# Holding back the first loads of SP's queue and moving four weight steps one to two page units later, in a one-core decoder step

## The chip, the cores and the metric

The kernel runs on one core of a Trainium2 chip. The metric is the device time of one execution in microseconds. One core has five engines with instruction streams of their own: PE (TensorE), DVE (VectorE), ACT (ScalarE), POOL (GpSimd) and SP (SyncE). SP and ACT issue transfers on hardware queues, POOL on a software queue (q0 in the profile). SP's queue is q1, ACT's is q10. All queues share the core's 16 DMA engines.

## The reference

One decoder layer for a prompt of 512 tokens and eight samples of 8 tokens, model width 1024, fp32. The part that matters here is its start:

```python
mod = silu(c) @ w_ada + b_ada                    # (9 rows, 6*1024): three pairs of shift, scale and gate
h = rmsnorm(x, ln1_g) * (1 + scale) + shift      # x: 512 + 64 tokens x 1024
q, k, v, ... = split(h @ w_in)                   # the projection
kc = compress(cache_k_cmp[page_table])           # 8 samples x 16 pages, k and v
     # per 16 rows: chunk @ w_ck1 -> silu -> @ w_ck2
```

Behind it come attention in three branches, a short convolution, the output projection and a SwiGLU block, which the change doesn't touch.

## The kernel before, in words

**The start.** The paged keys and values of the compression branch are 16 *page units* of 1 MB (eight samples, keys and values in turn). POOL gathers each unit with four indirect transfers of 256 KB (line 894) into one of four slots of the ring `cring` in the tile `arena`; a slot is free when DVE has transposed the unit that lay in it (`turned`). For each unit u, DVE transposes it (line 1608), PE multiplies it by the first compression weights (`compress_first`, line 2521, 16 records of 128x256), ACT copies half of the product, DVE adds the other half, ACT applies silu, and PE multiplies by the second weights (`compress_second`, line 2529), for which it comes back after the next unit's first product. PE's order is a list written out by hand in a loop over the 16 units: `compress_first(u)`, then whatever the tables hang on this unit, then `compress_second(u - 1)`.

**What hangs on the units.** `ADA_AT` names the unit behind whose first product PE does step kk of the product of silu(c) with the first 2048 columns of `w_ada` (`ada_step`, line 2482, eight steps of 128 rows, each reads one 1 MB block). `X_AT` names the units at which PE turns the five normalised token tiles (`turn_tokens`, line 2447): tiles 0 and 1 at unit 8, 2 and 3 at unit 9, 4 at unit 10. At unit 12 PE turns the finished modulation (`mod_turn`). DVE then modulates the tokens and the projection begins at 114 us.

**SP's queue.** SP is a list in program order, too. It first loads the five token tiles (four of 512 KB, one of 256 KB, line 768), then the eight 1 MB blocks of `w_ada` (line 720) into the four slots of the ring `wring`, then the blocks of `w_in` (line 752) into the same slots. `cache(sp, i)` makes SP wait until page unit i has landed; it is a means of ordering only, since no data pass from the pages to these loads. Blocks 0 to 3 of `w_ada` wait for a page unit each. The bias (256 KB, line 760) goes out behind block 3. Blocks 4 to 7 have no `cache` wait; block 4 + n waits until PE has done step n (`ada_read`) and its slot is free, and the first four blocks of `w_in` wait for steps 4 to 7 in the same way. The squares of the token tiles are taken on ACT at units 2 to 6.

The first block of `w_in` is cast by ACT (line 534) at unit 13.

Of the kernel before, what the change touches and what calls it, by code (L numbers as in the profile page):

```python
# [54 lines left out]
    [0, 128, 8, 80, 16, 512, 124, 124, 256, 512, 32, 900, 128]).tolist()  # L55


ADA_AT = {4: 0, 5: 1, 6: 2, 7: 3, 8: 4, 9: 5, 10: 6, 11: 7}


ADA1_AT = {2: 0, 3: 1, 5: 2, 6: 3, 8: 4, 9: 5, 11: 6, 13: 7}
# [196 lines left out]
def decoder_kernel(nc, a, o):  # L258
    at = plan_banks()
    chunks = plan_weights()  # L260
    chunk_of = {k: i for i, (k, _) in enumerate(chunks)}

    with ExitStack() as ctx:
# [213 lines left out]
        def ps(key):  # L477
            return bank[at[key][0]]

        def want_free(eng, key):  # L480

            b, n = at[key]
            if n:
                eng.wait_ge(bank_free[b], n)
# [11 lines left out]
        def fills(ins, key):  # L496
            ins.then_inc(bank_filled[at[key][0]], 1)
# [10 lines left out]
        def weights(pe, key):  # L508

            i = chunk_of[key]  # L510
            pe.wait_ge(w_loaded[i % WR], sum(loads_of(j) for j in range(i % WR, i + 1, WR)))
            return wch[:, i % WR]
# [5 lines left out]
        def cache(eng, i):  # L518

            eng.wait_ge(cache_loaded[slot_of(i)], 64 * (i // CR + 1) if i < 16 else 256 + 16 * (i // CR - 3))  # L520
            return cring[:, slot_of(i), :].rearrange("p (s n) -> p s n", s=16)

        def slot_of(i):

            return (i + 2) % CR

        def tok_rows(name_p, name_s, t):
            return a[name_p][0, 128 * t:128 * t + 128, :] if t < 4 else a[name_s].rearrange("b q d -> (b q) d")
# [36 lines left out]
        def down_job(j):  # L565

            n, i = divmod(j - NFT, 6)
            kc = DN_KC[n][i]
            return n, i, kc, 4 if kc < 5 else NFT - 20
# [5 lines left out]
        def reads_job(j):  # L575

            if j < NFT:
                return lambda eng: want_filled(eng, ("gu",) + FAST[-1])
            n, i, _, _ = down_job(j)
            return (lambda eng: eng.wait_ge(dn_read, 5 * n + i + 1)) if i < 5 else (  # L580
                lambda eng: want_filled(eng, ("dn", n, DN_ORDER[-1])))

        def job_parts(j):

            n, _, kc, nk = down_job(j)
            raw, parts, k0 = wch[:, chunk_of["dn", n, kc] % WR, 0:nk], [], 0
            his, los = dn_w[j % 2]
            for i, lo in enumerate(los):
                m = min(nk - k0, lo.shape[1] // 512)
                if m > 0:  # L590
                    hi = his[0][:, 512 * k0:512 * (k0 + m)]
                    parts.append([raw[:, k0:k0 + m]] + [z.rearrange("p (k c) -> p k c", k=m) for z in (hi, lo[:, 0:512 * m])])
                    k0 += m
            return parts
# [89 lines left out]
        def _(sp):  # L684
# [79 lines left out]
            for t in range(5):  # L764
                if t in (0, 1, 3):

                    cache(sp, (t + 1) // 2)
                sp.dma_start(xs[0:TM[t], t, :], tok_rows("x_prompt", "x_sample", t)).then_inc(x_loaded[t], 16)
            for i in range(WR):
                cache(sp, 3 + i)  # L770
                load(i)
            bias(0)
            for i in range(WR, done):
# [1669 lines left out]
        def _(pe):  # L2443
# [23 lines left out]
            def mod_turn(l):  # L2467
                key = ("mod", l)
                want_free(pe, key)
                want_emptied(pe, ("ada", l))  # L2470
                for c in range(4):
                    ins = turn(ps(key)[:, 128 * c:128 * c + 128], arows[:, 512 * l + 128 * c:512 * l + 128 * c + 128])
                fills(ins, key)

            def ada_step(g, kk):

                key = ("ada", g)
                if kk == 0:
                    want_free(pe, key)
                w = weights(pe, ("ada", g, kk))  # L2480
                for j in range(4):
                    ins = pe.matmul(ps(key)[32 * j:32 * j + 32, :], cT[:, 32 * kk:32 * kk + 32], w[:, j, :],  # L2482
                                    start=kk == 0, stop=kk == 7)
                if kk == 7:
                    fills(ins, key)
                else:
                    ins.then_inc(ada_read, 1)

            def turn_rows():
                pe.wait_ge(scrow_ready, 1)  # L2490
                want_free(pe, ("cT",))
                for k in range(8):
                    ins = turn(ps(("cT",))[:, 9 * k:9 * k + 9], scrow[:, 128 * k:128 * k + 128])
                fills(ins, ("cT",))
                pe.wait_ge(gains_loaded, 112)
                want_free(pe, ("rows",))
                fills(turn(ps(("rows",))[:, 0:52], rowb[:, :]), ("rows",))

            def position_rows():

                pe.wait_ge(comp_w_loaded, 160)
                want_emptied(pe, ("cT",))
                want_emptied(pe, ("rows",))
                for x in range(2):
                    want_free(pe, ("peb", x))
                ins = [None, None]
                for i in range(16):
                    for x in range(2):
                        ins[x] = pe.matmul(ps(("peb", x))[64 * x:64 * x + 64, 0:1], w1v[:, x, i % 8, i // 8, :], colT[:, 36 + i:37 + i],
                                           start=i == 0, stop=i == 15)  # L2510
                for x in range(2):
                    fills(ins[x], ("peb", x))

            def compress_first(u):
                n, key = (CH if u < 16 else PCH), ("pre", u)
                want_free(pe, key)
                pe.wait_ge(turned, u + 1)
                x = xcmp[u % 2 + (0 if u < 16 else 2)].rearrange("p (n s k e r) -> p s e k n r", s=4, k=2, e=2, r=32)
                dst = ps(key)[:, 0:2 * n].rearrange("p (k n r) -> p k n r", k=2, r=32)
                for j in range(8):  # L2520
                    ins = pe.matmul(dst, w1v[:, u % 2, j].rearrange("p r h -> p (r h)"), x[:, j // 2, j % 2], start=j == 0, stop=j == 7)  # L2521
                fills(ins, key)

            def compress_second(u):
                key, m, x = ("cmp", u), (NC if u < 16 else PNC), u % 2
                want_free(pe, key)
                pe.wait_ge(silu_ready, u + 1)
                for k in range(2):
                    ins = pe.matmul(ps(key)[0:m, 64 * k:64 * k + 64], slu[:, k, 0:m], w2[:, 64 * x:64 * x + 64],
                                    start=True, stop=True)  # L2530
                fills(ins, key)

            def turn_state():

                pe.wait_ge(conv_state_loaded, 16)
                want_free(pe, ("sconv",))
                for m in range(4):
                    ins = turn(ps(("sconv",))[:, 16 * m:16 * m + 16], stc[:, 128 * m:128 * m + 128])
                fills(ins, ("sconv",))

            def turn_tokens(t):
                pe.wait_ge(xn_ready, t + 1)
                for h in range(2):
                    key = ("xT", t, h)
                    want_free(pe, key)
                    for k in range(4):
                        f = 128 * (4 * h + k)
                        ins = turn(ps(key)[:, TM[t] * k:TM[t] * k + TM[t]], xs[0:TM[t], t, f:f + 128])
                    fills(ins, key)
# [7 lines left out]
            for u in range(16):  # L2557
                if u == 0:
                    turn_rows()
                    pe.wait_ge(comp_k_loaded, 128)  # L2560
                compress_first(u)
                if u == 0:
                    position_rows()
                if u in ADA_AT:
                    ada_step(0, ADA_AT[u])
                if u == 5:
                    turn_state()
                for t in X_AT.get(u, ()):
                    turn_tokens(t)
                if u == 12:  # L2570
                    mod_turn(0)
                if u:
                    compress_second(u - 1)
# [321 lines left out]
            for s in range(2, NST + LAG + 1):  # L2895
                if 2 <= s < NST:
                    prompt_scores(s)
                if s in CMP_TURN:
                    t = CMP_TURN[s]
# [7 lines left out]
                if s in CMP_VALUE:  # L2907
                    t = CMP_VALUE[s]
# [10 lines left out]
                if LAG <= s < NST + LAG:  # L2919
                    v = s - LAG  # L2920
                    t, _, gs = STEPS[v]
# [10 lines left out]
                if s > LAG:  # L2932
                    v = s - LAG - 1
                    t, br, gs = STEPS[v]
# [142 lines left out]
            for j in range(NFT, NFT + 12):  # L3077
                n, i, kc, nk = down_job(j)
# [74 lines left out]
```

## Time and profile before

| what | value |
|---|---|
| median of 3 runs | 890.17 us (888.61 to 890.68) |
| the profiled execution | 891.03 us, its span 889.2 us, so 1.83 us lie around the span |
| PE busy in the span | 846.4 us, 95% |
| DVE, ACT, POOL busy | 626.1, 374.3, 306.1 us |
| mean granted clock of TensorE | 0.986 |
| data moved by DMA | 138.83 MB, mean 156 GB/s |

Times in the rows are microseconds from the start of the span. A timeline row gives start, duration, engine, line, operation, the tile written and the tiles read, the count, and in brackets how long the engine had been idle before it and what ended that. Engine names with a q (SPq) are an engine's issue of a transfer.

### The profile page before, as it was taken

Reading aid. Unit: us, or ns where it says so; the run is one execution under the profiler, and the core shown is the slowest. Engines: PE = TensorE matmul, PEld = TensorE weight load, DVE = VectorE, ACT = ScalarE, POOL = GpSimd, SP = SyncE. Lnnn points to the kernel's source line nnn. Section 1 sums busy time; section 2 is a strip of 40 time slices with the busy share of each in tenths; the row PEclk is TensorE's granted clock in tenths of the full one; section 3 lists DMA queues with packets and bytes.
Section 4 is the critical chain, followed back from the end, with each engine's and each line's share of the span. In section 5 each row is a group of like instructions: output and inputs, shape, how many; then the busy total and the mean of one; then the engine's idle time right before and its main releaser. Section 6 shows DMA issues by size and latency. Waiting matters only on the chain.

```text
span 889.2 us, 16417 instructions
## 1 busy us (share of the span) xinstructions
PE 846.4 (95%) x6333; PEld 728.1 (82%) x6333; DVE 626.1 (70%) x1232; ACT 374.3 (42%) x754; POOL 306.1 (34%) x303
## 2 busy tenths in 40 slices
PE   3898999999989899999999989999999999999998
PEld 2776788999975667667677989999999999888886
DVE  3457773698758876685759898888999888434434
ACT  1242342221235447668625744444444445322320
POOL 6776100000022314445001167777777772000000
PEclk9899999999997999999999999999999999999999
DMA  8999622264468993961021914333333326222201
GB/s 234 353 372 393 233 64 90 71 216 163 147 230 328 399 370 118 310 181 42 1 65 78 237 49 123 100 96 91 93 92 95 90 95 211 95 95 95 77 1 53
DMA packets 89164, 138.83 MB, mean 156 GB/s; under 512 B 9268, under 2 KB 59988, under 8 KB 84799
## 3 DMA queue, kind: packets, MB, share of 16 engines
q1 hardware_dynamic: 74866, 96.26, 33.6%
q0 software_dynamic: 9376, 40.31, 12.3%
q10 hardware_dynamic: 4844, 1.21, 0.7%
q8 instruction: 51, 0.84, 0.4%
q14 instruction: 27, 0.21, 0.1%
HBM read 130.58 MB, written 11.31 MB: 160 GB/s over the span
## 4 chain that ended last, share of the span: by engine, by line
PE 78%; DVE 7%; DMA 5%; POOL 4%; issue 3%; ACT 3%; SPq 0%; DVEq 0%; ACTq 0%; POOLq 0%
PE bank L2453 19%; PE bank L2455 19%; PE bank L2454 19%; PE bank L2447 4%; POOL arena L894 3%; PE bank L2809 2%; DMA wring<-in_w_ada 2%; PE bank L2521 2%; PE bank L2941 2%; PE bank L2463 2%; PE bank L2462 2%; PE bank L2482 2%; PE bank L2973 2%; PE bank L2779 1%; DMA arena<-in_cache_k_slc,idx 1%
## 5 line engine op out<-in xcount | busy, mean ns | idle before, releaser
L2453 PE MATMUL bank<-s,ring_hi 128*128 128x288 f32 x620 | 184.6, 298 | 3.2 <-DVE ring_lo L537 3.2
L2454 PE MATMUL bank<-s,ring_lo 128*128 128x288 f32 x620 | 183.6, 296 | 0.0
L2455 PE MATMUL bank<-s,ring_hi 128*128 128x288 f32 x620 | 183.1, 295 | 0.0
L2453 PEld LDWEIGHTS bank<-s,ring_hi 128*128 128x128 f32 x620 | 116.9, 189 | 3.9 <-DVE ring_lo L537 3.8
L2455 PEld LDWEIGHTS bank<-s,ring_hi 128*128 128x128 f32 x620 | 117.5, 189 | 0.0
L2454 PEld LDWEIGHTS bank<-s,ring_lo 128*128 128x128 f32 x620 | 117.1, 189 | 0.0
L537 DVE TENSOR_TENSOR ring_lo<-mem,ring_hi 128x512 fp32r<-128x512 f32 x84 | 108.3, 1325 | 0.9 <-POOL mem L990 0.5
L537 DVE TENSOR_TENSOR dn_w<-wring,dn_w 128x2048 fp32r<-128x2048 f32 (+1 forms) x11 | 23.1, 2096 | 65.9 <-ACT dn_w L534 65.9
L903 POOL DMA_INDIRECT arena<-in_cache_k_slc,idx x8 | 7.9, 990 | 159.8 <-PE bank L2455 151.7
L2453 PE MATMUL bank<-dn_w,dn_hi 128*128 128x512 f32 x160 | 62.2, 389 | 0.0
L2454 PE MATMUL bank<-dn_w,dn_lo 128*128 128x512 f32 x160 | 62.2, 389 | 0.0
L2455 PE MATMUL bank<-dn_w,dn_hi 128*128 128x512 f32 x160 | 62.2, 389 | 0.0
L2453 PE MATMUL bank<-hhi,ws 128*128 128x288 f32 x192 | 56.8, 296 | 0.0
L2455 PE MATMUL bank<-h1hi,ws 128*128 128x288 f32 x192 | 56.6, 295 | 0.0
L2454 PE MATMUL bank<-h1hi,ws 128*128 128x288 f32 x192 | 56.5, 294 | 0.0
L534 ACT CAST dn_w<-wring 128x2048 fp32r<-128x2048 f32 (+1 forms) x11 | 19.3, 1757 | 83.0 <-PE bank L2455 83.0
L534 ACT CAST ring_hi<-mem 128x512 fp32r<-128x512 f32 x84 | 49.9, 617 | 6.5 <-POOL mem L982 2.3
L537 DVE TENSOR_TENSOR ring_lo<-wring,ring_hi 128x512 fp32r<-128x512 f32 x71 | 50.6, 718 | 0.5 <-ACT ring_hi L534 0.5
L982 POOL TENSOR_TENSOR mem<-wring 128x512 f32<-128x512 f32 x20 | 26.6, 1332 | 55.8 <-PE bank L2455 32.1
L534 ACT CAST ws<-wring 128x1024 fp32r<-128x1024 f32 (+2 forms) x18 | 21.8, 1245 | 48.4 <-PE bank L2463 27.2
L534 ACT CAST ring_hi<-wring 128x512 fp32r<-128x512 f32 x71 | 39.8, 616 | 0.0
L537 DVE TENSOR_TENSOR ws<-wring,ws 128x1024 fp32r<-128x1024 f32 (+2 forms) x18 | 25.9, 1468 | 18.2 <-ACT ws L534 18.0
(450 smaller groups left out, 2119.3 us busy)
## 6 DMA issues: line engine op xcount, KB each, us to landing
wring<-in_w_gu SPq DMA_DIRECT2D x44, 512.0 KB, 5.2
wring<-in_w_ada SPq DMA_DIRECT2D x16, 1024.0 KB, 10.3
wring<-in_w_in SPq DMA_DIRECT2D x10, 1024.0 KB, 5.2
wring<-in_w_down SPq DMA_DIRECT2D x10, 1024.0 KB, 5.1
wring<-in_w_ada SPq DMA_DIRECT2D x16, 512.0 KB, 8.7
proj<-in_x_prompt SPq DMA_DIRECT2D x4, 512.0 KB, 6.2
mem<-in_state_k_win POOLq DMA_DIRECT2D x8, 256.0 KB, 5.6
mem<-in_state_v_win POOLq DMA_DIRECT2D x8, 256.0 KB, 7.9
```

The costliest lines, as they stand in the source:

```text
L534: return copy(dst, src)
L537: return eng.tensor_tensor(dst, src, hi.bitcast(F32), ALU.subtract)
L894: pool.indirect_dma_start(cring[:, slot_of(i), 512 * n:512 * n + 512], None, a[name].rearrange("l n (c i s) k d -> (l n c i) (s k d)", i=4 ...
L982: ins = pool.tensor_tensor(dst, block_of(f, 0), block_of(f, 1), ALU.subtract)
L2447: return pe.transpose(dst, src, ident[0:P, 0:P])
L2453: pe.matmul(dst, sh, ml, start=first and k == 0, stop=False)
L2454: pe.matmul(dst, sl, mh, start=False, stop=False)
L2455: ins = pe.matmul(dst, sh, mh, start=False, stop=last and k == len(pairs) - 1)
L2462: pe.matmul(dst, s, ml, start=first and k == 0, stop=False)
L2463: ins = pe.matmul(dst, s, mh, start=False, stop=last and k == len(pairs) - 1)
L2482: ins = pe.matmul(ps(key)[32 * j:32 * j + 32, :], cT[:, 32 * kk:32 * kk + 32], w[:, j, :], start=kk == 0, stop=kk == 7)
L2521: ins = pe.matmul(dst, w1v[:, u % 2, j].rearrange("p r h -> p (r h)"), x[:, j // 2, j % 2], start=j == 0, stop=j == 7)
```

## The change

SP waits for later page units ahead of two token tiles and three of the four first blocks, and PE does steps 4, 5 and 6 one unit later.

| | before | after |
|---|---|---|
| token tile 0, 1, 2 | unit 0, unit 1, no wait of its own | the same |
| token tile 3 (and 4 behind it) | unit 2 | unit 3 |
| `w_ada` blocks 0, 1, 2, 3 | units 3, 4, 5, 6 | units 4, 5, 5, 6 |
| steps 0 to 3 on PE | units 4, 5, 6, 7 | the same |
| steps 4, 5, 6, 7 on PE | units 8, 9, 10, 11 | units 9, 10, 11, 11 |

```diff
-ADA_AT = {4: 0, 5: 1, 6: 2, 7: 3, 8: 4, 9: 5, 10: 6, 11: 7}
+ADA_AT = {4: (0,), 5: (1,), 6: (2,), 7: (3,), 9: (4,), 10: (5,), 11: (6, 7)}
...
             for t in range(5):
                 if t in (0, 1, 3):
-                    cache(sp, (t + 1) // 2)
+                    cache(sp, (0, 1, 1, 3)[t])
                 sp.dma_start(xs[0:TM[t], t, :], tok_rows("x_prompt", "x_sample", t)).then_inc(x_loaded[t], 16)
             for i in range(WR):
-                cache(sp, 3 + i)
+                cache(sp, (4, 5, 5, 6)[i])
                 load(i)
...
-                if u in ADA_AT:
-                    ada_step(0, ADA_AT[u])
+                for kk in ADA_AT.get(u, ()):
+                    ada_step(0, kk)
```

## Rows read from the trace of the kernel before

**Rows 1.** The page, part 1: busy time of each engine.
```profile
PE 846.4 (95%) x6333; PEld 728.1 (82%) x6333; DVE 626.1 (70%) x1232; ACT 374.3 (42%) x754; POOL 306.1 (34%) x303
```

**Rows 2.** Stages of 5 us: PE, PEld, DVE, ACT, POOL busy; PEclk; DMA share; GB/s.
```profile
30.00:35.00 5.00, 3.34 (x17) 2.60 (x15) 1.12 (x1) 1.39 (x3) 3.78 (x5) 0.99 1.02 306
35.00:40.00 5.00, 3.66 (x9) 2.97 (x10) 4.17 (x5) 1.55 (x3) 3.78 (x5) 0.50 1.03 401
40.00:45.00 5.00, 5.00 (x21) 4.01 (x20) 1.78 (x2) 1.70 (x3) 3.78 (x5) 0.82 1.02 406
```

**Rows 3.** PE's waits from 30 to 100 us: total, times, longest.
```profile
PE bank L2521 <- DVE mem L1608: 3.0, 1, 3.0
PE bank L2482 <- DMA wring<-in_w_ada: 2.7, 1, 2.7
```

**Rows 4.** Timeline of PE, 28 to 53 us.
```profile
32.69 0.65 PE L2529 MATMUL bank<-proj,arena 64*127 64x64 f32 x4
36.34 6.37 PE L2521 MATMUL bank<-mem 128*128 128x256 f32 x16 [3.00 <-DVE mem L1608]
...
43.22 3.72 PE L2521 MATMUL bank<-uvT,mem 128*128 128x256 f32 x16
...
52.10 1.06 PE L2482 MATMUL bank<-wring,cT 128*32 128x512 f32 x8
```

**Rows 5.** Timeline of PE, 58 to 85 us.
```profile
64.48 3.72 PE L2521 MATMUL bank<-uvT,mem 128*128 128x256 f32 x16
70.85 1.07 PE L2482 MATMUL bank<-wring,cT 128*32 128x512 f32 x8 [2.65 <-DMA wring<-in_w_ada]
71.85 1.97 PE L2447 MATMUL bank<-cst,proj 128*128 128x128 f32 x16
...
81.45 3.72 PE L2521 MATMUL bank<-uvT,mem 128*128 128x256 f32 x16
```

**Rows 6.** Timeline of DVE: units 3, 9 and 10 and the work ahead of unit 3.
```profile
29.03 0.41 DVE L1614 TENSOR_TENSOR arena<-arena,bank 64x254 f32<-64x254 f32 x1 [1.12 <-ACT arena L1061]
33.88 2.31 DVE L1608 STREAM_TRANSPOSE mem<-arena 128x2048 f32<-128x2048 f32 x1 [4.44 <-DMA arena<-in_cache_v_cmp,idq]
...
67.12 2.31 DVE L1608 STREAM_TRANSPOSE mem<-arena 128x2048 f32<-128x2048 f32 x1 [3.23 <-DMA arena<-in_cache_v_cmp,idq]
...
74.46 2.31 DVE L1608 STREAM_TRANSPOSE uvT<-arena 128x2048 f32<-128x2048 f32 x1 [0.35 <-DMA arena<-in_cache_k_cmp,idq]
```

**Rows 7.** Timeline of SP's issues: tiles 1 to 3, blocks 1, 2 and 4.
```profile
19.74 2.98 SPq L768 DMA_DIRECT2D proj<-in_x_prompt  x3
36.60 0.33 SPq L720 DMA_DIRECT2D wring<-in_w_ada  x1
41.79 0.33 SPq L720 DMA_DIRECT2D wring<-in_w_ada  x1
50.51 0.47 SPq L720 DMA_DIRECT2D wring<-in_w_ada  x1
```

**Rows 8.** DMA issues (count, KB each, median us to landing), issued 33.7 to 42.5, 46 to 76, 70 to 100 us.
```profile
wring<-in_w_ada SPq DMA_DIRECT2D x3, 1024.0 KB, 8.1
...
wring<-in_w_ada SPq DMA_DIRECT2D x5, 1024.0 KB, 20.3
...
wring<-in_w_in SPq DMA_DIRECT2D x4, 1024.0 KB, 17.1
```

**Rows 9.** The page queue (packets, MB, share of the engines), 35 to 50 and 55 to 70 us.
```profile
q0 software_dynamic: 890, 2.92, 50.4%
...
q0 software_dynamic: 571, 1.85, 35.7%
```

**Rows 10.** Timeline of POOL: the last gather of unit 3.
```profile
23.16 0.95 POOL L894 DMA_INDIRECT arena<-in_cache_v_cmp,idq  x1 [0.30 <-issue]
```

**Rows 11.** Timeline of ACT: the cast of w_in's first block.
```profile
97.66 1.88 ACT L534 CAST ws<-wring 128x2048 fp32r<-128x2048 f32 x1
```

## The prediction

> **What bounds the kernel now.** I read the busy times first: PE is busy 95% of the span [rows 1], so a start that ends earlier should carry through to the end, and only waits that PE itself has are worth removing. The stages come next. Around 35 us the granted clock is 0.50, the lower of the two levels (1.2 instead of 2.4 GHz), before it is back at full during the stage from 40 us [rows 2]. Then PE's own waits from 30 to 100 us: two entries, 3.0 us for DVE's transpose of a page unit and 2.7 us for a block of w_ada [rows 3]. The timelines place them. PE had finished the second product of unit 1 at 33.34, stood 3.00 us until the transpose of unit 3, and then needed 6.37 us at the low clock for a product that takes 3.72 at the high one [rows 4]. The second wait stands ahead of step 4 at unit 8, 2.65 us [rows 5]. Together PE lost 3.00 + (6.37 - 3.72) + 2.65 = 8.3 us there, and that is all that a change in this stage can return.
>
> The reader should see in DVE's timeline what lies behind the first loss: unit 3 had landed only at 33.88 [rows 6], 9.8 us behind the end of its last gather at 24.11 [rows 10]. SP issued tile 3 at about 22.4, with tile 4 behind it, just as unit 2 landed [rows 7]; gathers go out every 1.25 us, so unit 2's last one ended at 19.1, and unit 2 took 3.3 us from there. Unit 1 took 5.6 (its last gather ended at 14.1; tile 1 was issued on its landing at 19.74). What is different at unit 3 is 0.79 MB of tiles 3 and 4 in flight beside it.
>
> **The change part by part.**
>
> **Tiles 3 and 4 behind unit 3.** Without them unit 3 lands 3.3 to 5.6 us behind 24.1, at 27.4 to 29.7. I take 29.5, the slow end, as tiles 1 and 2 are still in flight. DVE can't transpose it before 29.44 anyway, when it is done with unit 1's sum [rows 6]; so the transpose runs from 29.5 to 31.8. PE gets to it at 33.34: wait gone, and the clock has nothing to fall for there. That gives 3.00 + 2.65 = 5.65. If unit 3 lands later than 31.0, the wait comes back; if as before, nothing is gained here (the other end). The tiles go out 7 us later than before, but ACT squares them at units 5 and 6, and unit 5's step stands at 52.10 [rows 4], over 20 us behind the issue. That is free.
>
> **Unit 4 and block 0.** Tiles 3 and 4 now fall on unit 4. Unit 4's last gather ends 5.0 us behind unit 3's, at 29.1. Between 5.6 us (unit 1) and the 7.5 us of before (it landed at 36.60, where block 1 was issued [rows 7]) it lands at 34.7 to 36.6; I take 35.4. Its transpose is done 2.3 later, at 37.7, and PE wants it at 33.3 + 3.6 + 0.6 = 37.5: a wait of 0.2 (0 to 1.4). Block 0 is issued on that landing and takes 8.1 us [rows 8], to 43.5. PE reaches step 0 at 37.7 + 3.65 = 41.35. So **a new wait of 2.2 us** (0.7 to 3.4), the largest cost of the change. Behind the waiting step on PE stand the second product of unit 3 and the first of unit 5, and ACT and DVE wait for those.
>
> **Blocks 1 and 2 both behind unit 5.** Unit 5 landed at 41.79 [rows 7]; I take 41.0. Block 1 lands at 49.1. Step 1 stood at 52.10 [rows 4] and would be reached 5.65 - 0.2 - 2.2 = 3.25 earlier, at 48.85: 0.25 of waiting (0 to 2). Block 2 is queued behind it. Pages and SP each got half of some 0.4 MB/us from 35 to 50 us (2.92 MB of pages in 15 us [rows 9]), so a block of 1.05 MB is about 5.2 us: it lands at 54.3, and step 2, a unit of 5.2 to 5.6 us behind step 1, is reached at 54.5. No wait (0 to 1.5). Block 3 follows 5.2 us behind, its step too. At unit 8 PE is 3.0 us earlier than before.
>
> **Steps 4 to 7.** The move itself costs nothing, the same matmuls run. Step 4 is now behind unit 9's first product. Taking it out of unit 8 removes the wait of 2.65 and, for the moment, the step of 1.0: unit 8's product starts at 64.48 - 3.0 = 61.5, ends at 65.15, the turns of tiles 0 and 1 (1.9) and the second product (0.6) end at 67.6, and unit 9 is wanted there. Its pages landed at 67.12 [rows 6]. I expect 66, 1.1 sooner, because SP's blocks 1 and 3 go out no sooner than before; its transpose ends at 68.3: **0.7 of waiting** (0 to 1.8). Step 4 is reached at 72. Block 4 landed at 70.8, 20.3 us behind its issue [rows 7, 8]; it is behind block 3 and the bias as before, so I leave it there, and it is hidden by unit 9's product; were it 2 us later, 0.8 would show. Unit 10 is wanted at 75.4 and landed at 74.46 before; 1.1 sooner and transposed in 2.3, it is ready at 75.7: **0.3** (0 to 1.4). Even with both units as before, unit 10's product would start at 76.8 instead of 81.45 [rows 5], 4.7 earlier with one step of 1.0 still to come, so 3.7 would remain. Steps 6 and 7 at unit 11 are reached around 86; block 7 is issued behind step 3, at about 61, and with 20.3 us it lands at 81.
>
> **Against the arbitration rule.** The page queue got 50.4% of the engines' time from 35 to 50 us, but 35.7% from 55 to 70, when SP had several blocks outstanding [rows 9]. The Trainium skill, "DMA: Bandwidth & Descriptors" (section "Queues, rings and completion order"), says that each DMA engine goes round-robin between the queue rows that have work, a packet at a time; by that rule the pages would keep half however many blocks SP has queued. The first stage agrees, the second doesn't. By the rule the 1.5 MB that came from 55 to 67.1 us at 0.123 MB/us would come at 0.195 in 7.6 us, unit 9 would land at about 63, the last two waits would be nothing and the gain 1.0 more. I go by the second stage's row.
>
> **w_in.** Its first block is issued behind step 4, at about 73 instead of 71.9, and takes 17.1 us [rows 8], to 90.1. ACT casts it at 97.66 [rows 11], then some 93. Cover of 3 us; without it, ACT's copies for unit 13 stand behind the cast. Nothing is booked.
>
> **Sum.** 8.3 - 0.2 - 2.2 - 0.25 - 0.7 - 0.3 = 4.65. From unit 12 on, modulation and projection follow in the same order, so the shift is kept. The profiled execution would take 891.03 - 4.65 = 886.4; the median of the runs shown is 0.86 below that execution, so **885.5** is the forecast.
>
> **The rivals.**
>
> *All waits hidden.* Unit 4 lands by 34 and its block within 7 us, unit 9 by 64: the gain is the whole 8.3, 881.9. For it: the pages are alone on the engines while SP waits. Against: block 0 would have to beat every landing in [rows 8]. 0.12.
>
> *Unit 3 stays late.* If its lag came from the engines and not from the tiles, only the 2.65 at unit 8 is gained: 887.5. Against it is unit 2's lag of 3.3 us. 0.12.
>
> *The clock falls at the new wait.* A wait of 3.00 us was followed by the low clock until about 41.6 [rows 2, 4], one of 2.65 wasn't [rows 5]. At 2.2 us and more ahead of step 0 it could fall again; 6.6 us at half speed cost 3.3, and 4.65 - 3.3 = 1.35 remain: 888.8. The Trainium skill, "TensorE: Matmul & The Clock Gate" (section "HAM oscillation — how this bites in real kernels"), has it that a wait for a transfer between bursts puts the array back to half clock each time; here one wait did and one didn't. 0.17.
>
> *Slower: two blocks at once land like blocks 4 to 6.* Those took about 20 us instead of 8 [rows 8], with several outstanding. If block 1, with block 2 right behind it, took 20.3 from 41.0, it would land at 61.3, step 1 would wait 12.2 more than booked, which hides the 1.0 booked at units 9 and 10: 6.5 lost, 896.7. It decides once block 1 lands after 54.7, 13.7 us behind its issue. Against: blocks 0 to 2 took 8.1 in the median [rows 8]. 0.08.
>
> **How the numbers follow.** The forecast has 0.42, the rivals 0.49; 0.09 is for a shift that is lost later on, where PE has other waits and falls of the clock. 0.2% is 1.8 us, about what a measurement of this kernel can tell from no change. Faster by more than that: 0.42 + 0.12 + 0.12 + 0.03 = 0.69. Within it: 0.17 + 0.02 = 0.19. Slower: 0.08 + 0.04 = 0.12. The range goes from all waits hidden, 881.5, to the low clock with 1.2 us more of waiting, 890.0, and leaves out the slower cases.
>
> **What would show it.** Right: unit 3's transpose at 29 to 31, PE's clock at 1.00 from 33 to 41, a wait of about 2 us ahead of step 0, none ahead of step 4 at unit 9, the projection beginning 4 to 5 us sooner. Wrong: unit 3 later than 31; a clock of 0.50 behind 41; step 1 waiting for block 1 beyond 50; unit 10's pages later than 75; or the projection sooner and the end not.

## The result and the profile after

The changed kernel is slower by 0.2%: median 893.65 us over 13 runs (891.57 to 895.03), the kernel before 891.43 over 13 runs beside it (888.61 to 893.53), ratio 1.0022 with a 95% interval of 1.0011 to 1.0032. 885.5 was forecast, with a range of 881.5 to 890.0. The table of the change and its diff show what was moved: tiles 3 and 4, blocks 0 and 1 (blocks 2 and 3 keep units 5 and 6), and steps 4, 5 and 6, each by one unit. The title and the sentence over that table say more than that. The profiled execution took 892.02 us, its span is 890.2. PE's work is the same [rows 1]:

```profile
PE 846.8 (95%) x6333; PEld 728.7 (82%) x6333; DVE 626.4 (70%) x1232; ACT 374.3 (42%) x754; POOL 306.7 (34%) x303
```

PE's waits from 20 to 100 us after the change (total, times, longest), to be held against [rows 3]:

```profile
PE bank L2521 <- DVE uvT L1608: 1.7, 1, 1.7
PE bank L2521 <- DVE mem L1531: 1.1, 1, 1.1
PE bank L2521 <- DVE mem L1608: 1.0, 1, 1.0
PE bank L2509 <- DVE colT L1531: 0.5, 1, 0.5
PE bank L2482 <- DMA wring<-in_w_ada: 0.2, 1, 0.2
```

Both old waits are gone, and five others stand there. The one of 0.5 us lies at 23 us, ahead of the stage that the prediction added up; behind it PE is 0.2 us later than in the trace of before. The timeline of PE after the change, answering to [rows 4, 5], places them:

```profile
33.49 3.72 PE L2521 MATMUL bank<-mem 128*128 128x256 f32 x16
...
41.69 1.07 PE L2482 MATMUL bank<-wring,cT 128*32 128x512 f32 x8 [0.25 <-DMA wring<-in_w_ada]
...
44.39 5.38 PE L2521 MATMUL bank<-mem 128*128 128x256 f32 x16 [1.05 <-DVE mem L1608]
...
63.89 5.38 PE L2521 MATMUL bank<-uvT,mem 128*128 128x256 f32 x16 [1.75 <-DVE uvT L1608]
...
72.73 3.72 PE L2521 MATMUL bank<-mem 128*128 128x256 f32 x16 [1.13 <-DVE mem L1531]
76.39 1.07 PE L2482 MATMUL bank<-wring,cT 128*32 128x512 f32 x8
...
95.23 0.60 PE L2447 MATMUL bank<-cst,arows 128*128 128x128 f32 x4
```

Unit 3's product (33.49) starts at once and runs at full clock: 2.85 us earlier than before, 5.5 us earlier at its end. Then the products of units 5 and 8 wait 1.05 and 1.75 us, and both take 5.38 instead of 3.72 us. The stages of 5 us say why (PEclk is the number behind POOL's busy time; compare [rows 2]):

```profile
35.00:40.00 5.00, 5.00 (x26) 4.14 (x25) 1.70 (x3) 2.39 (x6) 3.78 (x5) 1.00 1.00 338
...
45.00:50.00 5.00, 5.00 (x20) 3.71 (x22) 2.13 (x2) 1.51 (x4) 3.78 (x5) 0.71 1.02 415
...
65.00:70.00 5.00, 5.00 (x21) 4.10 (x21) 0.78 (x2) 0.88 (x2) 3.45 (x4) 0.67 1.02 403
```

From 35 to 40 us the clock is 1.00, where it was 0.50. But from 45 and from 65 us it is 0.71 and 0.67, the lower level in a part of each stage. Add up the other four waits and what the low clock cost (5.38 - 3.72 = 1.66, twice): 0.25 + 1.05 + 1.66 + 1.75 + 1.66 + 1.13 = 7.5 us lost, against 8.3 before and 3.65 forecast. The turn of the modulation at unit 12 stands at 95.23 and stood at 95.97, so 0.7 us are left of the gain, about what the two sums leave (8.3 - 7.5). From there to the end of the span it is 795.0 us after and 793.2 before, so that this execution as a whole is 1.0 us longer.

DVE's timeline after the change, units 3, 5, 8 and 9 (compare [rows 6]), shows what PE waited for:

```profile
29.64 2.31 DVE L1608 STREAM_TRANSPOSE mem<-arena 128x2048 f32<-128x2048 f32 x1
...
41.93 2.31 DVE L1608 STREAM_TRANSPOSE mem<-arena 128x2048 f32<-128x2048 f32 x1 [3.80 <-DMA arena<-in_cache_v_cmp,idq]
...
61.44 2.31 DVE L1608 STREAM_TRANSPOSE uvT<-arena 128x2048 f32<-128x2048 f32 x1 [5.18 <-DMA arena<-in_cache_k_cmp,idq]
...
70.19 2.31 DVE L1608 STREAM_TRANSPOSE mem<-arena 128x2048 f32<-128x2048 f32 x1 [4.41 <-DMA arena<-in_cache_v_cmp,idq]
```

Unit 3 is transposed 4.2 us sooner than before. Unit 9 comes 3.1 us **later**, 70.19 against 67.12. DVE was idle ahead of units 5, 8 and 9 until the pages landed: the page transfers bind here, not an engine. What competes with them is SP's queue. Its issues before, block 3 and blocks 5, 6 and 7, which [rows 7] leaves out:

```profile
49.46 0.33 SPq L720 DMA_DIRECT2D wring<-in_w_ada  x1
...
53.23 0.33 SPq L720 DMA_DIRECT2D wring<-in_w_ada  x1
...
58.80 0.33 SPq L720 DMA_DIRECT2D wring<-in_w_ada  x1
...
64.03 0.33 SPq L720 DMA_DIRECT2D wring<-in_w_ada  x1
```

Its issues after the change (compare [rows 7]):

```profile
41.85 0.80 SPq L720 DMA_DIRECT2D wring<-in_w_ada  x2
44.37 0.33 SPq L720 DMA_DIRECT2D wring<-in_w_ada  x1
45.43 0.47 SPq L720 DMA_DIRECT2D wring<-in_w_ada  x1
50.82 0.33 SPq L720 DMA_DIRECT2D wring<-in_w_ada  x1
56.40 0.33 SPq L720 DMA_DIRECT2D wring<-in_w_ada  x1
61.62 0.33 SPq L720 DMA_DIRECT2D wring<-in_w_ada  x1
```

These are blocks 1 and 2, 3, 4, 5, 6 and 7. Block 1 is 5.3 us later than before, but block 3 goes out 5.1 us sooner, at 44.37, block 4 5.1 us sooner, and blocks 5 to 7 2.4 us sooner each: four blocks and the bias go out within 4.1 us. What releases them is seen beside PE's rows: block 3 waits for unit 6, which came sooner, block 4 follows behind the bias, and blocks 5, 6 and 7 go out as steps 1, 2 and 3 end (the first of these runs from 49.69 to 50.75 us, block 5 goes out at 50.82). Blocks 4 to 7 land so late behind their issue:

```profile
DMA to landing us min/median/max: 19.0/21.5/24.1
```

From 50 to 70 us SP's queue and the page queue (packets, MB, share of the engines' time) have this; the page queue had 2.97 MB and 41.5% before:

```profile
q1 hardware_dynamic: 766, 4.87, 65.9%
q0 software_dynamic: 770, 2.52, 35.4%
```

The packets are even, 766 to 770. But one of SP's queue was 6.4 KB on average and one of the pages 3.3 KB, so even turns gave the pages a third of the time. The same holds for the stage from 55 to 70 us before, where the page queue had 571 packets [rows 9]:

```profile
q1 hardware_dynamic: 579, 3.49, 65.8%
```

### The profile page after: what moved, and what is told of

It reads as the page before. It is cut to its first block, busy times and chain, and to the rows that moved or that the text cites. A ratio compares the mean times of both kernels' runs of the same rounds, so it can differ in the third digit from the quotient of the medians.

```text
span 890.2 us, 16417 instructions
## 1 busy us (share of the span) xinstructions
PE 846.8 (95%) x6333; PEld 728.7 (82%) x6333; DVE 626.4 (70%) x1232; ACT 374.3 (42%) x754; POOL 306.7 (34%) x303
## 3 DMA queue, kind: packets, MB, share of 16 engines
q0 software_dynamic: 9376, 40.31, 12.5%
## 4 chain that ended last, share of the span: by engine, by line
PE 76%; DVE 8%; POOL 5%; DMA 4%; issue 4%; ACT 3%; DVEq 0%; POOLq 0%; ACTq 0%
PE bank L2453 18%; PE bank L2455 18%; PE bank L2454 18%; PE bank L2447 4%; POOL arena L894 3%; DMA arena<-in_cache_v_cmp,idq 3%; PE bank L2809 2%; PE bank L2521 2%; PE bank L2941 2%; PE bank L2462 2%; PE bank L2463 2%; PE bank L2482 2%; PE bank L2973 2%; DMA arena<-in_cache_k_slc,idx 1%; PE bank L2779 1%
## 5 line engine op out<-in xcount | busy, mean ns | idle before, releaser
L537 DVE TENSOR_TENSOR dn_w<-wring,dn_w 128x2048 fp32r<-128x2048 f32 (+1 forms) x11 | 23.1, 2097 | 65.8 <-ACT dn_w L534 65.8
L537 DVE TENSOR_TENSOR ring_lo<-wring,ring_hi 128x512 fp32r<-128x512 f32 x71 | 52.6, 747 | 0.5 <-ACT ring_hi L534 0.5
```

Source lines behind the costliest of these rows:

```text
L537: return eng.tensor_tensor(dst, src, hi.bitcast(F32), ALU.subtract)
```

## The experiments

**Theory.** The landing of units 8 and 9 sets this stage, and SP's blocks 4 to 7 set that landing. Those go out behind earlier pages and PE's steps, so whatever is gained early sends them out sooner, and the later pages give it back. **Rivals:** the moved steps cost the time by themselves (order on PE); blocks 1 and 2 both behind unit 5 cost it; or it is lost later, behind the start. Each ratio below is to the kernel before on the same chip, with its 95% interval.

**One part at a time.** Each part of the diff was put into the kernel before by itself.

> Only token tiles 3 and 4 behind unit 3; blocks and steps as before. Theory A (pages starve once SP has several w_ada blocks outstanding, and SP issues blocks 4 to 7 as soon as PE's steps let it): unit 3 lands by 30, PE's wait of 3.0 and the low clock behind it go, so at unit 4 PE is about 5 us sooner; blocks 4 to 7 go out that much sooner, units 8 to 10 land as late as before or later (unit 9 at 67 or later), and by unit 12 no more than 2.5 us are left. Time: 0.1 to 0.3% under the kernel before. Rival B (the tiles only move the crowd: unit 3 was late through something else): unit 3 lands at 33 or later and the time is the same. Rival C (the saved time is kept, what cost the changed kernel its gain were the held blocks or the moved steps): 4 us or more faster, 0.5%.

> Only w_ada blocks 0 to 3 behind units 4, 5, 5, 6; tiles and steps as before. Theory A: PE is not sooner, since the wait for unit 3 stays; block 3 onward go out as before, so units 8 and 9 land as before and the time is within 0.2%. Rival C (two blocks behind one unit are the harm): a wait of PE ahead of step 1 or 2, or units 7 to 9 later than before by 2 us or more, and 0.2 to 0.5% slower.

> Only steps 4 to 7 at units 9, 10, 11, 11; SP's waits as before. Theory A: blocks 4 to 7 go out as before, so units 8 and 9 land as before (unit 9 at 67); the wait of 2.65 ahead of step 4 is gone, unit 9's product starts when its transpose is done, at 69.5, and by unit 12 PE is 2.5 to 3.7 us sooner: 0.3 to 0.4% faster. Rival D (what is saved at the start is lost further along, in the attention and SwiGLU stages): PE is sooner at unit 12 by as much, but the time is within 0.15% of before.

**And two parts.**

> Tiles 3 and 4 behind unit 3 and steps 4 to 7 at units 9, 10, 11, 11; blocks 0 to 3 behind units 3, 4, 5, 6 as before. Theory A (what counts is how many w_ada blocks are outstanding while units 6 to 9 are under way): SP has no more of them outstanding than with the tiles alone, so the time is that of the tiles alone, 0.1 to 0.3% under the kernel before; moving the steps adds nothing, as PE then waits for units 8 and 9. Rival F (moving the steps costs by itself, because w_in's loads go out later): 0.1% or more over the kernel before.

> Tiles 3 and 4 behind unit 3 and blocks 0 to 3 behind units 4, 5, 5, 6; steps 4 to 7 at units 8 to 11 as before. Theory A: blocks 1 to 4 and the bias go out within some 4 us around 42 to 46, as in the changed kernel, units 8 and 9 land as late as there (60 and 69 or later), and the time is that of the changed kernel, 0.1 to 0.3% over the kernel before. Rival F: without the moved steps it is as fast as the tiles alone, 0.1 to 0.3% under the kernel before.

| parts of the change | median us | ratio | unit 8 / unit 9 transposed | turn at unit 12 |
|---|---|---|---|---|
| tiles | 889.40 | 0.9986 (0.9970 to 1.0001) | 60.58 / 69.71 | 93.89 |
| blocks | 892.86 | 1.0009 (0.9991 to 1.0027) | 59.19 / 68.34 | 92.73 |
| steps | 891.89 | 1.0004 (0.9989 to 1.0018) | 61.43 / 69.76 | 95.27 |
| tiles, steps | 893.45 | 1.0003 (0.9989 to 1.0017) | 64.06 / 71.60 | 96.88 |
| tiles, blocks | 892.89 | 1.0013 (0.9996 to 1.0030) | 61.74 / 70.34 | 94.52 |
| all three (the change) | 893.65 | 1.0022 (1.0011 to 1.0032) | 61.44 / 70.19 | 95.23 |

Every interval but that of the whole change includes 1. The tiles tend to help (1.2 us), and blocks or steps beside them take that back; the intervals of the tiles and of the whole change don't overlap. Theory A foretold the tiles (0.1 to 0.3% faster), and tiles with blocks came out on its side. It missed twice: the steps alone were to be 0.3 to 0.4% faster, and tiles with steps 0.1 to 0.3%, and both took the time of before.

The times of the traces are those of one execution each; that of the blocks alone was the fastest of its runs, 888.33. In these six traces a distance repeats. From the transpose of unit 9 to the turn at unit 12 it is 24.2 to 24.4 us with step 4 at unit 8 (tiles, blocks, both) and 25.0 to 25.5 with step 4 at unit 9 (steps, tiles and steps, all three). About the one step of 1.0 us lies between them. In the trace of the tiles PE still waits 0.74 us for unit 9 behind step 4, so there the step costs nothing; behind unit 9 it comes on top. In the two traces of the kernel before the distance is 28.9 and 26.4 us, since PE had other work to finish when unit 9 came. So the order on PE can cost up to 1 us where unit 9's pages bind, which is argued from single traces; it is not the forecast gain.

**Second executions of both kernels.**

> The kernel before, unchanged, for a second trace. If the landing of unit 3 at 33.9 and the low clock behind it belong to the kernel, they are there again. If they were one draw of how the transfers fell out, unit 3 lands at 31 to 32, as with the held blocks or the moved steps alone, and PE's loss at unit 3 is under 1 us; then the loss that the tiles could give back was counted too high.

> The changed kernel, unchanged, for a second trace. Theory A: unit 3 is there in time again, and units 8 and 9 land at 60 to 63 and 69 to 72 again, with the page queue at about a third of the engines' time from 50 to 70 us.

The second execution of the kernel before took 893.45 us (span 891.6). DVE's timeline, units 3 and 8:

```profile
31.93 2.31 DVE L1608 STREAM_TRANSPOSE mem<-arena 128x2048 f32<-128x2048 f32 x1 [2.03 <-DMA arena<-in_cache_v_cmp,idq]
...
62.31 2.31 DVE L1608 STREAM_TRANSPOSE uvT<-arena 128x2048 f32<-128x2048 f32 x1 [7.06 <-DMA arena<-in_cache_k_cmp,idq]
```

PE's timeline there, unit 8:

```profile
64.77 6.28 PE L2521 MATMUL bank<-uvT,mem 128*128 128x256 f32 x16 [4.60 <-DVE uvT L1608]
```

In the first trace of before unit 8 was transposed here:

```profile
58.59 2.30 DVE L1608 STREAM_TRANSPOSE uvT<-arena 128x2048 f32<-128x2048 f32 x1
```

These are the most telling rows. In this execution of the *unchanged* kernel PE waited only 0.59 us for unit 3, and its product ran at full clock: the loss that the change was to remove wasn't there. PE was ahead, SP's block 4 went out at 45.76 instead of 50.51, and unit 8 came at 62.31 instead of 58.59. PE then stood 4.60 us there, with a low clock behind it. Waits and low clock add up to 8.0 us, against 8.3, and the turn at unit 12 is at 96.09 against 95.97. It is the same loss, at another unit. Blocks 4 to 7 go out at 45.76, 48.60, 54.17 and 59.65 here, after the change at 45.43, 50.82, 56.40 and 61.62. So the change sends them sooner only in comparison with the first trace of before, in which unit 3 was late.

The second execution of the changed kernel took 892.17 us: unit 3 at 30.19, units 8 and 9 at 63.48 and 70.92, the turn at 96.07. A third was taken later, 893.34 us:

> The changed kernel once more. If its 0.2% lies in the first stage, unit 12's turn is later than in the two traces of before (96.0 and 96.1) by up to 2 us; if behind it, the turn is at 95 to 96 and the way from there to the end is longer than 793.2 to 795.5 us.

DVE's timeline of it, units 8 and 9:

```profile
64.86 2.31 DVE L1608 STREAM_TRANSPOSE uvT<-arena 128x2048 f32<-128x2048 f32 x1 [7.74 <-DMA arena<-in_cache_k_cmp,idq]
...
72.96 2.31 DVE L1608 STREAM_TRANSPOSE mem<-arena 128x2048 f32<-128x2048 f32 x1 [3.74 <-DMA arena<-in_cache_v_cmp,idq]
```

The turn is at 98.74, 2.65 us later than the later one of before; unit 3 was transposed at 31.77 only, and a product ahead of it took 5.41 us. Over the three, unit 9 is at 70.2 to 73.0 after the change and at 67.1 and 69.7 before it. From the turn to the end it is 792.8 to 795.0 us after and 793.2 and 795.5 before, and 792.6 to 795.6 over the 18 traces of all kernels here. Nothing speaks for the rival that the time is lost later. But this rest differs by 3.0 us between executions, more than the 2.2 us in question, so the traces don't show where the 0.2% lies.

**Blocks 4 to 7 held back.** If the theory holds, it helps to tie these blocks to the late pages as well. The waits on PE's steps and on the slots stay.

```diff
             for i in range(WR, done):
+                if i < 8:
+                    cache(sp, (7, 8, 9, 10)[i - WR])
                 load(i)
```

On top of the change:

> The changed kernel, and blocks 4 to 7 also wait for a page unit: 7, 8, 9 and 10. Theory A: with fewer blocks outstanding units 8 and 9 land some 3 to 5 us sooner than in the changed kernel (61.4 and 70.2 there), the waits of 1.75 and 1.1 and the low clock behind the first go, and PE is at unit 12 some 3 us sooner than in the changed kernel: 0.3% faster than it, 0.2 to 0.4% faster than before. Rival E (the bias behind block 3 keeps some engines behind, not the blocks): units 8 and 9 land as in the changed kernel and the time is that of the changed kernel or worse, since the blocks come later.

By itself, in the kernel before:

> The kernel before with one thing added: blocks 4 to 7 of w_ada wait for page units 7, 8, 9 and 10. Theory A (PE's steps release blocks 4 to 7, so whatever PE gains early sends them out early, and the pages of units 8 and 9 pay it back): the hold breaks that loop by itself. Units 8 and 9 land at 57 to 60 and 65 to 67, the page queue has more than half of the engines' time from 50 to 70 us, and the time is 0.2 to 0.4% under the kernel before; PE waits ahead of step 4 at unit 8, which costs up to 2 us of it. Rival G (the hold is only worth something together with the tiles, the held first blocks and the moved steps): within 0.15% of the kernel before.

On top of the change: 887.68 us, ratio 0.9965 (0.9952 to 0.9977). By itself: 888.64, ratio 0.9964 (0.9948 to 0.9980). With the hold on top of the change, DVE's timeline has units 8 and 9 at

```profile
58.86 2.31 DVE L1610 STREAM_TRANSPOSE uvT<-arena 128x2048 f32<-128x2048 f32 x1 [1.90 <-DMA arena<-in_cache_k_cmp,idq]
65.84 2.31 DVE L1610 STREAM_TRANSPOSE mem<-arena 128x2048 f32<-128x2048 f32 x1 [2.63 <-DMA arena<-in_cache_v_cmp,idq]
```

and the page queue from 50 to 70 us

```profile
q0 software_dynamic: 1228, 4.04, 57.9%
```

4.04 MB of pages instead of 2.52 in the same 20 us, and unit 9 is 4.4 us earlier. Blocks 4 to 7 go out later but land in 8.3 to 12.5 us instead of 19.0 to 24.1, so no step waits for them; one wait of PE is left from 30 to 100 us, 2.2 us at unit 7, with the low clock behind it. The order on PE is that of the change, so the rival that this order costs the time falls as the main cause. The hold is worth as much without the change as with it.

**Half of the bytes.** This kernel is the changed one, but of blocks 4 to 7 only the first 1024 of 2048 columns are loaded. It leaves out half of their bytes, and the other half of the product reads what the slot held.

```diff
+                        if n == 0 and kh >= 4:
+                            w = 1024
```

> The changed kernel with half of the bytes of w_ada's blocks 4 to 7: only their first 1024 columns are loaded, so the products with the other columns use what lay in the slot. Theory A: 2 MB less beside the pages of units 6 to 10; units 8 and 9 land 2 to 5 us sooner than in the changed kernel (61.4 and 70.2 in one trace of it, 63.5 and 70.9 in the other), PE's waits for them go, and the time is 0.4 to 0.8% under the kernel before. Rival H (units 8 and 9 are late through their own gathers or the bias): they land as in the changed kernel, and the time is within 0.2% of its.

887.99 us, ratio 0.9951 (0.9934 to 0.9967); the pages get 3.99 MB from 50 to 70 us (57.7% of the engines' time), unit 9 is transposed at 67.52 and isn't waited for by DVE. No order and no wait was changed here. So it is the bytes of these blocks that hold the pages back. Unit 8 misses the expectation: it comes at 63.23, behind a late unit 7 (56.17), not 2 to 5 us sooner. This trace is the slowest of the kernel's six runs, so the gain is read from the median of the runs and not from it.

**The bias.** It goes out ahead of block 4, 256 KB from a source whose slowest dimension is 4 (four rows, each read for 32 partitions). Here it goes out behind block 7, first in the changed kernel, then in the kernel before.

```diff
-            bias(0)
             for i in range(WR, done):
                 load(i)
+                if i == 7:
+                    bias(0)
```

> The changed kernel with the 256 KB bias load behind block 7 instead of behind block 3. Theory A: the bias is 0.26 of the 5.5 MB that SP has put out by 62 us; units 8 and 9 land at most 1 us sooner and the time is within 0.15% of the changed kernel's (0.1 to 0.3% over the kernel before). Rival E (the bias, which comes from four rows that are each spread to 32 partitions, holds some of the engines up, and all that is behind it with them): units 8 and 9 land 3 us sooner or more, blocks 4 to 7 take 8 to 12 us instead of 19 to 24, and the time is 0.2% or more under the kernel before.

> The kernel before with the bias load behind block 7 instead of behind block 3. Theory A (the number of blocks outstanding): units 8 and 9 land as before and the time is within 0.15% of before. Theory E (the bias holds some engines up): blocks 4 to 7 land 10 to 14 us behind their issue instead of about 20, step 4 at unit 8 doesn't wait, and the time is 0.2 to 0.4% under the kernel before. As the late bias gave 0.4% to the changed kernel, I expect something between, 0.1 to 0.3%.

> The changed kernel with the late bias once more. Theory E: blocks 4 to 7 take 10 to 14 us again, and unit 12's turn is 1 to 3 us sooner than in the changed kernel's traces; theory A: it is at 95 to 96.

Changed kernel: 890.13 us, 0.9980 (0.9966 to 0.9993). Kernel before: 889.05, 0.9976 (0.9960 to 0.9991). In the changed kernel blocks 3 to 7 land in 9.2 to 14.0 us, where blocks 4 to 7 took 19.0 to 24.1; in the kernel before, the blocks issued from 45 us on land in 9.3 to 12.6 us, and took about 20 us [rows 8], and step 4 doesn't wait there. So the long landing time came with the bias and not only from the number of blocks. In the trace of the change, block 3, issued at 44.37 ahead of the bias, lands in 12.8 us, and block 4, issued at 45.43 behind it, in 24.1. Neither expectation for the changed kernel fits as a whole: landing and time are as theory E has it, the pages as theory A, for they are no sooner. Their queue has 36.4 and 39.3% of the engines' time from 50 to 70 us in the two traces. Where the gain of the changed kernel shows in its traces stays open: unit 9 is at 70.44 there, and 69.35 in the second trace (892.60 us), the turn at 95.50 and 95.15, the early end of what the three traces without the edit show.

**Paced throughout.** Blocks 0 to 7 behind units 4, 5, 6, 7, 8, 9, 10 and 10, the tiles as in the change, the bias behind block 7, or, in the second kernel, behind block 3 as before.

```diff
-ADA_AT = {4: (0,), 5: (1,), 6: (2,), 7: (3,), 9: (4,), 10: (5,), 11: (6, 7)}
+ADA_AT = {4: (0,), 5: (1,), 6: (2,), 8: (3,), 9: (4,), 10: (5,), 11: (6, 7)}
...
-                cache(sp, (4, 5, 5, 6)[i])
+                cache(sp, 4 + i)
...
+                if i < 8:
+                    cache(sp, (8, 9, 10, 10)[i - WR])
```

> All of SP's first loads paced by the pages: tiles 3 and 4 behind unit 3, blocks 0 to 7 behind units 4, 5, 6, 7, 8, 9, 10, 10, the bias behind block 7, steps at units 4, 5, 6, 8, 9, 10, 11, 11. Theory A: one or two blocks outstanding at any time, units 7, 8 and 9 land at 49 to 51, 55 to 58 and 62 to 65, PE waits no more than 2 us in all, and is at unit 12's turn at 90 to 92 instead of 96: 0.4 to 0.7% under the kernel before, and faster than with the first hold. If blocks come late instead, PE waits ahead of a step and the time is that of the first hold or worse.

> All of SP's first loads paced by the pages as in the paced kernel, but with the bias back behind block 3, now behind unit 7. Theory A: one more transfer of 256 KB beside units 8 and 9, and the time stays within 0.1% of the paced kernel's (0.5% under the kernel before). Theory E: units 8 to 10 land 2 us later or more, blocks 4 to 7 take 15 us or more, and 0.2 to 0.4% of the paced kernel's gain is gone.

886.46 us, ratio 0.9949 (0.9933 to 0.9966), and 886.50, 0.9945 (0.9923 to 0.9966). Both are faster than the kernel before and, by their ratios, than the changed one. Against the hold alone the intervals overlap. PE's waits from 30 to 100 us with the late bias are one row:

```profile
PE bank L2485 <- DMA wring<-in_w_ada: 1.5, 1, 1.5
```

And DVE's timeline, units 8 and 9:

```profile
56.51 2.31 DVE L1611 STREAM_TRANSPOSE uvT<-arena 128x2048 f32<-128x2048 f32 x1 [1.66 <-DMA arena<-in_cache_k_cmp,idq]
60.78 2.30 DVE L1611 STREAM_TRANSPOSE mem<-arena 128x2048 f32<-128x2048 f32 x1
```

Unit 9 is 9.4 us earlier than after the change and waits for no page any more; the blocks whose landing is recorded take 7.3 to 8.8 us, and the turn at unit 12 is at 89.44. With the bias behind block 3, PE waits five times, 3.3 us in all, and the turn is at 91.66. The times of the runs are the same, so with blocks that don't pile up the place of the bias made no difference to them.

## Why the prediction was wrong, point by point

**Unit 3: right as a step, wrong as a price.** It was transposed at 29.64 (29.5 booked), and 5.5 of the 5.65 us came back by the end of its product. But 3.00 + 2.65 was the price of one execution. In the second trace of before, and in those of blocks alone, steps alone, the hold alone and the kernel before with a late bias, unit 3 is transposed at 31.0 to 31.9 without the change of the tiles, and PE waits 0.6 us or less for it. Such an execution has next to nothing to give there. With the tiles held, unit 3 came at 29.6 to 31.8.

**Step 0: mis-sized.** 2.2 us were booked, 0.25 measured. Unit 4 had landed by 32.59, when block 0 was issued, instead of 35.4.

**Step 1 and unit 5.** Step 1 didn't wait (0.25 booked). Unit 5 landed at 41.85, as before, and PE was there early: 1.05 of waiting and 1.66 of low clock, which had no term.

**The step that failed** is that the sum took PE 3 us earlier to units 8 and 9 and left the pages where the trace of before had them, or sooner. It stands in the prediction for unit 9: "I expect 66, 1.1 sooner, because SP's blocks 1 and 3 go out no sooner than before". Block 3 went out 5.1 us sooner, because unit 6 was there at 44.37 instead of 49.46 (and at 44.70 in the second trace of before, where PE waited just 0.59 us for unit 3), and block 4 right behind it; blocks 5 to 7 followed PE's earlier steps. Unit 9 came at 70.19, 4.2 us later than booked, and cost a wait of 1.13 (0.7 booked). Unit 8's product was to start at 61.5 with no wait; its pages came at 61.44, 2.85 us later than before, and that cost 1.75 + 1.66. With unit 5's 1.05 + 1.66, terms put at nothing are 6.1 of the 7.5 us lost. The prediction left the pages in place though it knew from [rows 8, 9] that blocks 4 to 7 are what slows them, and from the code that earlier pages and PE's steps release those. The hold kernels show this in its place: with blocks 4 to 7 tied to the pages, unit 9 came at 65.84 and 63.61. So the pair of traces has a gain of 0.7 us ahead of unit 12 instead of 4.65; that the runs are 0.2% slower on top of that isn't explained.

**"The move itself costs nothing"** failed by up to 1.0 us: true while step 4's wait for its block bound, not once unit 9's pages did. The wait ahead of step 4 did go (2.65 to 0).

**The arbitration rule: misread.** Its outcome by the prediction, unit 9 at 63, didn't come: from 50 to 70 us the pages had 35.4%, 35.6% and 35.3% in the three traces of the changed kernel. But the prediction took turns "a packet at a time" for halves of the time. By packets the turns were even where it saw a disagreement, 571 to 579 from 55 to 70 us before and 770 to 766 after. From 35 to 50 us, where it saw agreement, they weren't: 890 packets of the pages [rows 9] to 432 of SP's queue. The pages reached half of the time there because SP's queue took fewer turns:

```profile
q1 hardware_dynamic: 432, 3.15, 51.9%
```

From 50 to 70 us a share of half came only when SP's blocks were spread out (50.0, 50.7, 52.0 and 57.9% in the four kernels that pace or hold them) or halved (57.7%).

**The rivals.** "The clock falls at the new wait" was right in kind, at units 5 and 8 instead of step 0. "Two blocks at once land like blocks 4 to 6" didn't happen: blocks 1 and 2 landed 7.2 and 11.1 us behind their issue, and no step from 1 on waited. A slower time, to which the prediction gave 0.12, came, but not in this way.

**Left open.** Where in the execution the 0.2% lies, and how it divides between the blocks sent together and the moved steps: adding either to the tiles costs 1.5 to 2.4 us in the ratios, with overlapping intervals.

## What to carry to other kernels

A load that is released by its consumer's progress runs ahead when the consumer does; in a stretch where the DMA engines are full, that can hand an early gain back at the next transfer on the path. Tie prefetches to the stream that binds as well, not only to the engine that reads them: that alone was worth 0.36% here, where the change that was to remove visible waits cost 0.2%. And don't price a change by a wait seen in one execution: take a second trace, and ask what lands last if the engine were there sooner.

## What the runs showed of the hardware

- Short waits were often followed by the lower clock level, but the length of the wait alone didn't decide it. After waits of 1.05 and 1.75 us PE's next product took 5.38 instead of 3.72 us, after 2.18 (hold on the change) 5.38, after 4.60 us 6.28. After 1.13 us (unit 9, above), 1.06 (steps alone), 1.76 (hold alone) and 2.77 (the late bias's second trace) it took 3.69 to 3.72, with a granted clock of 1.00. The wait of 2.65 us ahead of step 4 had no such sequel either [rows 5].
- The page queue and SP's queue moved nearly the same number of packets where SP's queue had the most to send: 571 and 579, 770 and 766. Their shares of the engines' time were 35.7 and 65.8%, 35.4 and 65.9%.
- A transfer of 256 KB ahead of the blocks went with landing times of 19 to 24 us instead of 9 to 14 for the 1 MB blocks behind it. The Trainium skill, "DMA: Bandwidth & Descriptors" (section "Why a DMA increments its semaphore by 16 and not by 1"), says that a DMA is spread over the largest number of engines, up to 16, that divides the slowest dimension of both access patterns. By that the bias, with 4, would lie on 4 engines and the blocks behind it would wait for these. The landing times agree, and so do the packets in the trace of the change: the 128 packets of 2 KB that are the bias stand from 54.5 to 65.0 us, never more than four at a time, while of the blocks' packets 16 and more do. Which engines they are on isn't shown.
- Whole executions of one kernel differ by up to 7 us on one chip (888.04 to 895.08 us over 23 runs of the kernel before), with unit 3 transposed at 31.9 and 33.9 us in two traces of it.
